# Differential attention of a two-layer streaming encoder: value projection inside the prompt steps, half tiles of the output projection between the sample batches, and new orders at both ends

## What is computed

```python
h = rmsnorm(x, ln_mix[0])
aq, ak, av, bq, bk, bv, bg = split(h @ w_in_even)        # 1024 -> 7 x 512 columns
# A: differential attention, 4 heads, two score maps each
s = einsum("bqhcd,bkhcd->bchqk", q, k) * 64 ** -0.5 + bias ; chunk-causal mask
p = softmax(s) ;  w = p[:, 0] - lam * p[:, 1] ;  o_a = w @ v
o_a = head_rms(o_a) * subln * 0.8
# B: retention over the rotated bq, bk and bv, gated by silu(bg)
x = x + concat(o_a, o_b) @ w_out_even                    # "out0", 1024 -> 1024
# then cross-attention into a memory, gated MLP with a convolution,
# layer 1 (gated linear attention in place of A and B), the same again, final rmsnorm
```

## Time and profile before

| | |
|---|---|
| median of 3 runs | 2141.8 us (2141.14 to 2144.89) |
| profiled execution, its own time | 2141.79 us |
| span of its trace | 2140.0 us |
| PE busy | 2055.0 us (96%) |
| PE weight loads | 1805.9 us (84%) |
| DVE busy | 982.9 us (46%) |
| ACT busy | 761.9 us (36%) |
| POOL busy | 199.0 us (9%) |
| mean transfer rate | 103 GB/s |

### The profile page before, as it was taken

The page is one execution under the profiler, slowest core; times in us unless marked ns, Lnnn a source line. Parts: engine busy times, 40 slices in busy tenths (PEclk is TensorE's granted clock), DMA queues, the critical chain, the costliest instruction groups (busy, mean ns, idle before and its releaser), DMA issues.

```text
span 2140.0 us, 30512 instructions
## 1 busy us (share of the span) xinstructions
PE 2055.0 (96%) x12366; PEld 1805.9 (84%) x12366; DVE 982.9 (46%) x1650; ACT 761.9 (36%) x1314; POOL 199.0 (9%) x460
## 2 busy tenths in 40 slices
PE   7999869999999999999999999999999999999997
PEld 6889647898679999999978888789777999999996
DVE  5452463434545434444442458643454453443443
ACT  3222352434434332232333446233533333223232
POOL 2011211000100000000010124110010000000001
PEclk9999889999999999999999999999999999999999
DMA  6323313224822122222212211533482222222221
GB/s 196 103 94 109 131 59 119 89 80 167 314 82 80 60 79 80 89 79 79 79 59 76 79 40 45 194 126 109 153 315 68 79 71 78 71 88 79 79 79 53
DMA packets 111048, 219.94 MB, mean 103 GB/s; under 512 B 6994, under 2 KB 52350, under 8 KB 110844
## 3 DMA queue, kind: packets, MB, share of 16 engines
q1 hardware_dynamic: 89920, 143.80, 20.3%
q0 software_dynamic: 20416, 72.09, 9.8%
q10 hardware_dynamic: 576, 2.10, 0.2%
HBM read 201.03 MB, written 18.24 MB: 102 GB/s over the span
## 4 chain that ended last, share of the span: by engine, by line
PE 91%; DVE 4%; ACT 2%; issue 1%; DMA 1%; POOL 0%; SPq 0%; ACTq 0%; DVEq 0%; POOLq 0%
PE bank L746 15%; PE bank L748 14%; PE bank L747 14%; PE bank L810 7%; PE bank L806 7%; PE bank L808 7%; PE bank L805 5%; PE bank L807 5%; PE bank L809 5%; PE bank L1150 1%; PE bank L769 1%; PE bank L1167 1%; PE bank L1107 1%; PE bank L1191 1%; ACT sA L1612 1%
## 5 line engine op out<-in xcount | busy, mean ns | idle before, releaser
L1951 DVE TENSOR_TENSOR w_lo<-raw,w_hi 128x1024 fp32r<-128x1024 f32 x265 | 319.6, 1221 | 582.9 <-ACT w_hi L1461 578.8
L1461 ACT ACTIVATE w_hi<-raw 128x1024 fp32r<-128x1024 f32 x265 | 274.7, 1053 | 271.1 <-PE bank L748 216.0
L746 PE MATMUL bank<-w_hi,hT_lo 128*128 128x512 f32 x720 | 288.5, 401 | 6.8 <-DVE x L1993 3.7
L806 PE MATMUL bank<-hT_hi,w_lo 128*128 128x384 f32 (+1 forms) x856 | 289.3, 338 | 0.0
L808 PE MATMUL bank<-hT_lo,w_hi 128*128 128x384 f32 (+1 forms) x856 | 289.3, 338 | 0.0
L810 PE MATMUL bank<-hT_hi,w_hi 128*128 128x384 f32 (+1 forms) x856 | 289.3, 338 | 0.0
L748 PE MATMUL bank<-w_hi,hT_hi 128*128 128x512 f32 x720 | 281.8, 391 | 0.0
L747 PE MATMUL bank<-w_lo,hT_hi 128*128 128x512 f32 x720 | 281.3, 391 | 0.0
L805 PE MATMUL bank<-hT_hi,w_lo 128*128 128x256 f32 (+1 forms) x856 | 239.7, 280 | 0.0
L807 PE MATMUL bank<-hT_lo,w_hi 128*128 128x256 f32 (+1 forms) x856 | 239.1, 279 | 0.0
L809 PE MATMUL bank<-hT_hi,w_hi 128*128 128x256 f32 (+1 forms) x856 | 239.0, 279 | 0.0
(11 more groups left out here) (359 smaller groups left out, 3013.4 us busy)
## 6 DMA issues: line engine op xcount, KB each, us to landing
raw<-w_ffn_gate SPq DMA_DIRECT2D x44, 512.0 KB, 4.0
raw<-w_ffn_up SPq DMA_DIRECT2D x44, 512.0 KB, 5.1
raw<-w_ffn_down SPq DMA_DIRECT2D x22, 1024.0 KB, 5.0
kcX<-cache_mem_k POOLq DMA_DIRECT2D x16, 1024.0 KB, 6.3
vcX<-cache_mem_v POOLq DMA_DIRECT2D x16, 1024.0 KB, 7.0
raw<-w_in_even SPq DMA_DIRECT2D x14, 1024.0 KB, 5.2
raw<-w_in_odd SPq DMA_DIRECT2D x12, 1024.0 KB, 5.2
raw<-w_cq SPq DMA_DIRECT2D x8, 1024.0 KB, 7.3
```

Source lines behind the costliest of these rows:

```text
L746: pe.matmul(out, wl, xh, start=first, stop=False)
L806: pe.matmul(ob, wl, hT_hi[:, k, HA:TOK], start=f, stop=False)
L1461: act.activation(w_hi[:, g % W_SLOTS, 0:n], raw[:, q % 2, UNIT * i:UNIT * i + n], ACT.Copy).then_inc(*hi_made.mark(c, u))
L1951: dve.tensor_tensor(w_lo[:, s, 0:n], raw[:, q % 2, UNIT * i:UNIT * i + n], flat(w_hi[:, s, 0:n]), ALU.subtract).then_inc(*lo_made.mark(c, u))
```

## The change

- Value tiles 1 to 4 no longer stand ahead of the attention; each is cut into parts of 3, 3 and 2 of its 8 k (`VALUE_KS`), one part in each of steps 0 to 2, 4 to 6, 9 to 11, 14, 15 and behind the last step (`VALUE_PARTS`).
- `scores`, `maxima` and `exps` run two steps ahead; `sA` has three buffers; `weigh` stands behind the transpose.
- The `mixB` transposes go into turns 0 to 4 of the sample loop, and the first half tiles of `("out0", 0)` (`out_part`, 12 matmuls) into turns 4, 5, 6, 8 and 9 (`PAST_FILL`). The rest follows the loop.
- The weight units of `out0` are made in the loop's turns 1 to 3; DVE copies `akT` in between the units of `("in0", 2)`; on POOL the bias loads go ahead of the stores of `ak`, and the stores of `av` behind the loop. Several tiles change their address.
- Start: SP loads every tile of `x`, and only one row of the gain, which PE spreads over the 128 partitions; the first weight load is cut in two; ACT and DVE go through tile 0 first; PE transposes tile j + 1 behind k = 5 of tile j.
- End: SP issues the stores; the last tile's squares, scaling and store are cut in halves.

```diff
+HEAD_STEPS = [(t, h) for t in range(TP) for h in range(H)]
+VALUE_KS = [range(0, 3), range(3, 6), range(6, KT)]
+VALUE_PARTS = {s + i: (t, i) for t, s in ((1, 0), (2, 4), (3, 9), (TP, 14)) for i in range(len(VALUE_KS))}
+
+PAST_FILL = {4: (0, 0), 5: (0, 1), 6: (1, 0), 8: (1, 1), 9: (2, 0)}
...
-        sA = at("sA", 51200, [P, 2, 2, 512])
+        sA = at("sA", 51200, [P, 3, 2, 512])
...
+                    if between and k == 6:
+                        between()
...
+            pe.wait_ge(*pool_done.at("ones"))
+            pe.wait_ge(*gain_in.at("mix0"))
+            for n in range(2):
+                out = aux.open(pe, "gain", n)
+                pe.matmul(out[:, :], ones_row[:, :], gain_row[:, 512 * n:512 * n + 512], start=True, stop=True).then_inc(*aux_full.mark("gain", n))
...
-            for t in range(1, T):
-                proj_tile(("in0", 2), "mix0", t)
-            for t in range(T):
-                pe.wait_ge(*dve_done.at("ret_out", t))
-                to_mixed("mixB", t, 1, mixB[:, t, :])
...
+            def value_part(t, i):
+
+                c = ("in0", 2)
+                out = lin.bank(c, t) if i else lin.open(pe, c, t)
+                for k in VALUE_KS[i]:
+                    wait_unit(c, k // 2)
+                    cols = slice(512 * (k % 2), 512 * (k % 2) + 512)
+                    wh, wl = weight(c, k // 2, True)[:, cols], weight(c, k // 2, False)[:, cols]
+                    ins = three(out[:, :], hT_lo[:, k, P * t:P * t + P], hT_hi[:, k, P * t:P * t + P], wl, wh, k == 0, k == KT - 1)
...
             scores(0, 0)
-            for n, (t, h) in enumerate(seq):
-                if n + 1 < len(seq):
-                    scores(*seq[n + 1])
-                if n:
-                    weigh(n - 1, *seq[n - 1])
+            scores(0, 1)
+            for n, (t, h) in enumerate(HEAD_STEPS):
+                if n + 2 < len(HEAD_STEPS):
+                    scores(*HEAD_STEPS[n + 2])
+                if n in VALUE_PARTS:
+                    value_part(*VALUE_PARTS[n])
                 transpose_w(n, t, h)
                 if h == 3 and t >= 1:
                     pe.wait_ge(*dve_done.at("A_out", t - 1))
                     to_mixed("mixA", t - 1, 0, oaA[:, (t - 1) % 2, :])
-            weigh(len(seq) - 1, *seq[-1])
+                if n:
+                    weigh(n - 1, *HEAD_STEPS[n - 1])
+            value_part(*VALUE_PARTS[len(HEAD_STEPS)])
+            weigh(len(HEAD_STEPS) - 1, *HEAD_STEPS[-1])
...
+                if s < T:
+                    if s == 0:
+                        pe.wait_ge(*dve_done.at("ret_out", TP))
+                    to_mixed("mixB", s, 1, mixB[:, s, :])
...
+                if s in PAST_FILL:
+                    t, i = PAST_FILL[s]
+                    if i == 0:
+                        pe.wait_ge(*hT_made.at("mixA", t, 0))
+                        pe.wait_ge(*hT_made.at("mixB", t, 1))
+                    out_part(("out0", 0), t, i)
...
+            for t, i in ((2, 1), (3, 0), (3, 1)):
...
+                out_part(("out0", 0), t, i)
+            pe.wait_ge(*dve_done.at("A_out", TP))
+            to_mixed("mixA", TP, 0, oaA[:, TP % 2, :])
+            pe_done.after("mixed", 0)
+            for w, half in (("mixA", 0), ("mixB", 1)):
+                pe.wait_ge(*hT_made.at(w, TP, half))
+            proj_out(("out0", 0), TP)
...
+                if n in VALUE_PARTS and VALUE_PARTS[n][1] == len(VALUE_KS) - 1:
+                    value_copy(VALUE_PARTS[n][0])
+                if h == 0:
+                    if t >= 2:
+                        mixed_hi("mixA", t - 2, 0)
+                    if t:
+                        head_copy(act, link, t - 1)
+                if n + 2 < len(HEAD_STEPS):
+                    exps(n + 2, *HEAD_STEPS[n + 2])
...
+            scaled("mix0", 0)
+            split_lo(CHUNKS[0], [0])
+            halves("mix0", 0)
+            split_lo(CHUNKS[0], [1, 2])
+            scaled("mix0", 1)
+            split_lo(CHUNKS[0], [3])
+            halves("mix0", 1)
...
+                if s < T:
+                    mixed_lo("mixB", s, 1)
+                if s == 1:
+                    a_tail(TP - 1)
+                if s == 2:
+                    mixed_lo("mixA", TP - 1, 0)
+                if 1 <= s < 4:
+                    split_lo(("out0", 0), [s])
+                if s in PAST_FILL and PAST_FILL[s][1]:
+                    add_x(("out0", 0), PAST_FILL[s][0], 0)
...
-            for t in range(T):
-                norm_rstd("final", [t])
-                pool.wait_ge(*xn_made.at("final", t))
-                dst = io["o_y_p"][P * t:P * t + P, :] if t < TP else io["o_y_s"]
-                pool.dma_start(dst, xn[:, NORM_TILE[("final", t)] % 2, :]).then_inc(*put[f"y{t % 2}"].mark(t))
+            norm_rstd("final", range(T - 1))
```

More of the change, by code:

```diff
@@ L462, in _ @@
                     gains(before[c])
+                if q == 1:
+                    load_x(1)
+                if q == 2:
+                    for t in range(2, T):
+                        load_x(t)
                 if q >= 2:
@@ L770, in norm_tile, with proj_tile @@
                     ins.then_inc(*aux_full.mark("nT", nm, t, half))
-            def proj_tile(c, what, t, tiles=T, lo=hT_lo, hi=hT_hi):
+            def proj_tile(c, what, t, tiles=T, lo=hT_lo, hi=hT_hi, between=None):
                 wait_hT(what, t)
@@ L976, in _, with out_part @@
                     to_mixed("mixA", t - 1, 0, oaA[:, (t - 1) % 2, :])
-            weigh(len(seq) - 1, *seq[-1])
+                if n:
+                    weigh(n - 1, *HEAD_STEPS[n - 1])
+            value_part(*VALUE_PARTS[len(HEAD_STEPS)])
+            weigh(len(HEAD_STEPS) - 1, *HEAD_STEPS[-1])
             pe_done.after("attA_p")
+            def out_part(c, t, i):
+                out = lin.bank(c, t) if i else lin.open(pe, c, t)
+                for k in range(4 * i, 4 * i + 4):
+                    wait_unit(c, k // 2)
+                    cols = slice(512 * (k % 2), 512 * (k % 2) + 512)
+                    ins = three(out[:, :], hT_lo[:, k, P * t:P * t + P], hT_hi[:, k, P * t:P * t + P],
+                                weight(c, k // 2, False)[:, cols], weight(c, k // 2, True)[:, cols], k == 0, k == KT - 1)
+                if i:
+                    ins.then_inc(*lin_full.mark(c, t))
             def fold_w(b):
@@ L1024, in _ @@
             pe.wait_ge(*pool_done.at("fold", 1))
+            pe.wait_ge(*dve_done.at("akT", TP))
             for s in range(NB + 3):
@@ L1047, in proj_out @@
                 ins.then_inc(*lin_full.mark(c, t))
-            def out_part(c, t, i):
-                out = lin.bank(c, t) if i else lin.open(pe, c, t)
-                for k in range(4 * i, 4 * i + 4):
-                    wait_unit(c, k // 2)
-                    cols = slice(512 * (k % 2), 512 * (k % 2) + 512)
-                    ins = three(out[:, :], hT_lo[:, k, P * t:P * t + P], hT_hi[:, k, P * t:P * t + P],
-                                weight(c, k // 2, False)[:, cols], weight(c, k // 2, True)[:, cols], k == 0, k == KT - 1)
-                if i:
-                    ins.then_inc(*lin_full.mark(c, t))
             def norm_behind(nm, product, following, lag=1):
@@ L1070, in norm_behind @@
                 cols_pair(nm, following, 1)
-            def mix_out(cs, halves, sample, nm, following):
-                for t in range(T):
-                    if t == 2:
-                        sample()
-                    for w, half in halves:
-                        pe.wait_ge(*hT_made.at(w, t, half))
-                    proj_out(cs[0], t)
-                norm_behind(nm, lambda t: proj_out(cs[1], t), following)
             def rest(l):
@@ L1531, in rows_done @@
                 act_done.after(*mark)
-            def load_x(t):
-                src = io["x_prompt"][P * t:P * t + P, :] if t < TP else io["x_sample"]
-                act.dma_start(x[:, t, :], src).then_inc(*x_in[t].mark(t))
-            load_x(1)
-            for t in range(T):
-                norm_tile("mix0", "in", t)
-                if t + 2 < T:
-                    load_x(t + 2)
+            square("mix0", "in", 0)
+            for n in range(2):
+                act.wait_ge(*aux_full.at("gain", n))
+                act.activation(gain[:, 512 * n:512 * n + 512], aux.bank("gain", n)[:, :], ACT.Copy).then_inc(*aux_a.mark("gain", n))
+            split_hi(CHUNKS[0], [0, 1])
+            halves("mix0", 0)
+            square("mix0", "in", 1)
+            split_hi(CHUNKS[0], [2, 3])
+            for t in range(2, T):
+                square("mix0", "in", t)
+                halves("mix0", t - 1)
+            halves("mix0", T - 1)
             for j, (kind, t) in enumerate(RET_TILES):
@@ L1610, in exps @@
                 for c in range(2):
-                    s = sA[:, n % 2, c, 0:P * (t + 1)]
-                    act.activation(s, s, ACT.Exp, bias=small[:, n % 2, 2 + c:3 + c], accum_out=small[:, n % 2, 4 + c:5 + c]).then_inc(*act_done.mark("eA", t, h, c))
```

(15 more changed lines are left out.)

255 lines of the change are left out of this document (160 added, 95 removed).

## The result

The changed kernel takes 2112.53 us (median of four runs, 2112.05 to 2113.73), the kernel before 2142.82 in the same comparison: a ratio of 0.9861, 95% interval 0.9848 to 0.9874, or 30 us. The forecast was 2111, range 2099 to 2123.

A forecast was written before the change was run, and what follows sets the result against it. The prediction took PE's work plus PE's holes to bound the kernel. Its terms -28.4 - 1.8 + 3.7 - 2.9 - 1.8 sum to -31.2, so 2141.8 becomes 2110.6, say 2111, range 2099 to 2123.

The forecast's parts named there:

- Item 1: Attention stretch: value tiles woven into steps and lookahead two make it 58.6 us against 87.0, -28.4, with 53.5 of PE work.
- Holes 5.1: Attention stretch: estimated PE idle time that stays, at the start and at steps 7, 8, 11 and 12 to 14.
- plus one weight unit of 1.2 us: Attention stretch: DVE's load counted as 39 us for the steps and this one unit.
- Item 2: DVE copies each `akT` tile before three weight units, so PE's 1.8 us wait goes: -1.8, between 0 and -1.8.
- Item 3: Sample loop to the projection's first half: T + 69.8 against 66.15, +3.7 (-5 to +8), with +4 for the clock's fall.
- sure by a rule: Loop turns 0 to 3: the skill page on short idles between matmul groups on cycling banks makes the clock's fall sure.
- Item 4: Start: first product at 11.8 us, 5.4 earlier, less transposes (0.9) and waits (1.6) given back: -2.9, between 0 and -5.
- Item 5: End: early half square, DVE scaling in halves and SP's stores bring the last issue to about 2131.5: -1.8, -1 to -3.
- Rival B: Sample loop pays nothing: clock stays up, additions fit in DVE's waits, item 3 becomes -5, time 2101; chance 0.20.
- C: Attention keeps its pace: the chain per step stays the limit, stretch 67 us, loop 4 more, time 2123; chance 0.15.
- D: Slower: clock stays at 1.2 GHz through the attention and the loop's head, 2161 at half throughout; chance 0.05.
- E: No change: value tiles only push steps apart, and loop and start give back what is won; chance 0.03.

The follow-up runs named there:

- values_ahead: Changed kernel with value tiles 1 to 4 whole ahead of the attention again, lookahead of two kept: ratio 0.9924 to the kernel before.
- look_one: Changed kernel with a lookahead of one in scores, maxima and exps, value parts still woven into the steps: ratio 0.9908 to the kernel before.
- keys_first: Changed kernel with POOL's load of the keys of sample 2 ahead of the root for tile 3 of the attention's norm: ratio 0.9856 to the kernel before.
- unit_and_keys: Changed kernel with the edit of keys_first and DVE's weight unit 0 of `out0` one attention step later: ratio 0.9845 to the kernel before.
- old_start: Changed kernel with the whole start as before (loads, gain, orders of ACT and DVE, place of PE's transposes): ratio 0.9868 to the kernel before.
- old_end: Changed kernel with the end as before (POOL issues stores; last tile's squares, scaling and store whole): ratio 0.9873 to the kernel before.
- transposes_ahead: Changed kernel with only PE's start order as before, transposes of tile j + 1 ahead of the products of tile j: ratio 0.9862 to the kernel before.

## Why the prediction was right

- *What bounds: PE's work plus its holes, in the attention stretch.* Shown: values_ahead and look_one lengthen just this stretch, by 15.1 and 11.2 us (their loops stay at 68.2 and 68.3).
- *Item 1, PE work 53.5 us* measured 54.0. *Holes 5.1* measured 7.5. By place: the start 1.5 (measured 0.4), steps 7 and 8 0.8 (0.6 at step 7, and 0.8 for a bank of `ofA` at step 9, which I had not seen), step 11's bank 1.3 (1.16), steps 12 to 14 1.5 (1.34). The step that was wrong in size is "plus one weight unit of 1.2 us": I counted it as DVE's load and not as an instruction that waits with the chain queued behind it. It made 3.1 us of hole, and the clock of 0.64 in the window 242.04:246.76 behind it.
- *Item 2, `akT`*: -1.8 forecast, and the wait of 1.80 is gone whole.
- *Item 3, the loop pays +3.7*: it paid 1.8. Turn 4 ended at T + 24.2 against T + 24.8, the wait ahead of the last tile was 1.48 against 1.5; the turns behind took 27.7 against 25.4. The 4 us for the clock on top did not come on top: the lower clock came in turns 2 and 3, inside the 24.2, and was over by turn 4. The hole ahead of it was not a wait for DVE, as I had said, but for a load queued on POOL; keys_first shows DVE's queue right behind it. So the 24.2 came out without its first cause, and 2.3 us too little for the later turns stood against 4 too much for the clock: luck. "It has no hole to fill from the fourth turn on" is wrong: without the fill turns 4 to 10 have 6.8 us of waits. The old turn of 3.46 us has 0.36 of hole, but the new turns have more; which of the additions makes it was not separated. DVE also makes a fourth weight unit in the loop, in turn 8 (1.23 us at 329.23), that the sum does not have. The prediction also called the fall of the clock sure by a rule; unit_and_keys went through the loop at 1.00.
- *Item 4, the start, -2.9*: first product at 13.28 and not 11.8 (the gain's matmuls take 3.75 us, and `xn` is done at 9.73). The mark behind it is 0.8 us ahead of old_start's, less than its spread. The step that failed is the list of what is given back: it has nothing for the longer time at the lower clock and comes to 2.5 us, where 3.1 were lost.
- *Item 5, the end, -1.8*: -2.6, all of it by old_end. The forecast had the last issue 1.2 us earlier and so 0.6 for the halved store; measured are 1.5 and 1.1.

Against the marks the forecast is off by +1.9, +3.1, -1.9 and -0.8 us, and -0.4 in the rest, which leaves 1.9 in the sum: the mechanism was right, and that the time came within 2 us is in part errors of both signs. Of the signs named in advance, the waits for `sA` below 6 us, the wait of about 1.5 us ahead of the last `out0` tile and the lower clock in turns 1 to 3 came true; the stretch of 61.5 us is just above the 57 to 61, the first product at 13.28 just behind 13, and of the waits for DVE in turns 1 to 3 only 0.45 us was there.

Rival B wanted a clock that stays up and additions that fit in DVE's waits. The changed kernel has 0.73 and 0.69 in two windows of the loop, and even unit_and_keys, at 1.00 all through, has a loop of 67.0 us, more than the 66.2 before and far from B's 61. C is excluded by the 5.0 us of waits for `sA`, D by the clock of 0.97, E by the time.

## What to carry to other kernels

A chain over several engines that leaves PE idle costs its waits and the slower work behind them; independent matmuls cut to the size of the hole, and one more step of lookahead, each took about half of it here, and neither replaced the other. Look for instructions queued ahead of the chain's next link that wait for a third engine or are long: here a weight unit on DVE, a load on POOL, copies and squares on ACT. Where one wait ends as another begins, removing the first shows the second: price the edit by the second. Before you read a difference of one or two us out of two traces, look how far the same mark lies apart in kernels that have the same code up to it.

## What the hardware showed that I had not expected

What a wait costs at the lower clock is not the same from one execution to the next. In transposes_ahead and old_start the attention's code is that of the changed kernel, and PE waits 3.1 us at step 5 in all three. Their stretches:

```profile
222.00:282.99 60.99, 52.91 (x298) 38.54 (x297) 40.67 (x166) 35.52 (x105) 6.58 (x10) 1.00 0.11 39
221.44:284.27 62.83, 55.55 (x297) 40.22 (x296) 40.72 (x166) 35.30 (x105) 6.58 (x10) 0.95 0.10 36
```

The clock is 1.00 in the first, 0.97 in the changed kernel and 0.95 in the second, and PE is busy for 52.9, 54.5 and 55.6 us with the same matmuls: between nothing and an estimated 3 us for one wait (1 less 0.95, times 62.8). It is the same at the start. Eleven kernels have the new start, with the first product at 13.28 to 13.51 us, and their first matmul of under 0.5 us stands between 16.41 (old_end) and 19.54 (values_ahead). Rows of values_ahead:

```profile
19.19 0.51 PE L787 MATMUL bank<-w_lo,hT_hi 128*128 128x512 f32 x1
19.54 0.40 PE L788 MATMUL bank<-w_hi,hT_hi 128*128 128x512 f32 x1
```

Their marks at the `akT` transposes go with it: 220.42 and 221.99, the first and the last of the eleven. In the three kernels whose first product comes later, at 17.20 (before), 17.24 and 18.64, the lower clock ends 3.1, 2.7 and 1.4 us behind it, against 3.1 to 6.0 in the eleven: part of the lead of an earlier product is spent at the lower level.

The level also follows late. Behind the wait of 3.84 us in turn 2 the matmuls were slow to about 296 us, though PE was not idle (0.69 in that window). Yet keys_first stayed at 1.00 over 10.96 us with PE busy for only 6.91 of them:

```profile
283.35:294.31 10.96, 6.91 (x75) 5.02 (x73) 8.90 (x22) 6.04 (x14) 3.41 (x5) 1.00 0.55 160
294.31:300.12 5.81, 5.30 (x59) 3.87 (x59) 4.40 (x12) 3.40 (x7) 0.88 (x2) 0.71 0.74 233
```

and fell in the piece behind, where PE was busy for 5.30 of 5.81. unit_and_keys had the same waits up to there and did not fall at all.
